# First block: the second half of `down` and the first slot pair after it, run for the context tokens and then for the latent ones

## What is computed

```python
for l in range(2):
    lat = lat + 0.5 * ml[2] * swiglu(modulate(lat, norm_ffn1_g[l], ml[0], ml[1]), *ffn1)
    cx  = cx  + 0.5 * mc[2] * swiglu(modulate(cx,  norm_ffn1_g[l], mc[0], mc[1]), *ffn1)
    # token mixer on modulate(..., norm_mix_g[l], m[3], m[4]): projection w_in (14 slots of
    # 256 columns), gated MLP and bidirectional recurrence, projection w_out, residual
    lat = lat + ml[5] * out_lat        # cx likewise, in layer 0 only
    # second feed-forward like the first; cx in layer 0 only
modulate(x, g, shift, scale) = rmsnorm(x, g) * (1 + scale) + shift
swiglu(h, w1, w3, w2)        = (silu(h @ w1) * (h @ w3)) @ w2
ml[j], mc[j] = the nine parts of silu(cond) @ w_ada[l] + b_ada[l], for latent and context
log_lb, log_rest, kept = logarithms of the recurrence's lower bounds (from two parameter vectors)
```

## Time and profile before

| what | value |
|---|---|
| median of 3 runs | 2869.01 us (2867.65 to 2870.35) |
| profiled execution, its own time | 2868.01 us |
| its span in the trace | 2866.2 us |
| mean granted clock of TensorE | 0.962 of full |
| TensorE busy with matmuls | 2667.0 us (93%), 16745 of them |
| VectorE / ScalarE / POOL busy | 41% / 37% / 24% |
| DMA | 375 MB, mean 131 GB/s |

### The profile page before, as it was taken

One profiled execution on the slowest core, in us unless ns is written; L12 is line 12 of the kernel. 1 busy time (PEld: TensorE's weight loads), 2 busy tenths in 40 slices (PEclk: granted clock), 3 DMA queues, 4 the chain that ended last, 5 costly groups with the idle time before them and its releaser, 6 DMA issues. The chain is left out here.

```text
span 2866.2 us, 42736 instructions
## 1 busy us (share of the span) xinstructions
PE 2667.0 (93%) x16745; PEld 2321.4 (81%) x16745; DVE 1177.1 (41%) x1766; ACT 1068.2 (37%) x1474; POOL 688.5 (24%) x276
## 2 busy tenths in 40 slices
PE   6999898999889999989999989889999589996999
PEld 3888686988868888768888688779989489995999
DVE  3222224237642222242222356743354636634644
ACT  2322233535333222243222346445454344443433
POOL 0222121220012222212222213024434024440343
PEclk8999999999999999989999999999999789997999
DMA  5343353330023333434333424035555025551454
GB/s 228 133 168 138 125 145 114 122 132 1 30 103 139 133 132 132 147 105 145 132 132 132 168 85 162 6 118 176 178 201 190 30 96 180 181 177 44 149 188 148
DMA packets 57279, 375.37 MB, mean 131 GB/s; under 512 B 6159, under 2 KB 10919, under 8 KB 12872
## 3 DMA queue, kind: packets, MB, share of 16 engines
q1 hardware_dynamic: 56092, 371.58, 36.3%
q10 hardware_dynamic: 1068, 2.11, 0.6%
HBM read 370.51 MB, written 3.16 MB: 130 GB/s over the span
## 5 line engine op out<-in xcount | busy, mean ns | idle before, releaser
L1317 POOL TENSOR_TENSOR WL<-RAW,WH 128x1024 fp32r<-128x1024 f32 x272 | 688.3, 2530 | 2164.9 <-ACT WH L972 2164.9
L972 ACT ACTIVATE WH<-RAW 128x1024 fp32r<-128x1024 f32 x544 | 545.6, 1050 | 1075.0 <-PE PSA L512 1067.2
L1340 DVE TENSOR_TENSOR WL<-RAW,WH 128x1024 fp32r<-128x1024 f32 x272 | 346.7, 1275 | 1279.2 <-ACT WH L972 1279.1
L510 PE MATMUL PSA<-HH,WH 128*128 128x256 f32 (+1 forms) x2400 | 817.9, 341 | 25.3 <-DVE HL L1423 23.5
L511 PE MATMUL PSA<-HL,WH 128*128 128x256 f32 (+1 forms) x2400 | 807.9, 337 | 0.0
L512 PE MATMUL PSA<-HH,WL 128*128 128x256 f32 (+1 forms) x2400 | 806.5, 336 | 0.0
L510 PEld LDWEIGHTS PSA<-HH,WH 128*128 128x128 f32 x2400 | 459.8, 192 | 89.9 <-issue 43.2
L510 PE MATMUL PSA<-GH,WH 128*128 128x256 f32 (+1 forms) x1536 | 506.2, 330 | 7.0 <-DVE GL L1358 7.0
L511 PE MATMUL PSA<-GL,WH 128*128 128x256 f32 (+1 forms) x1536 | 498.8, 325 | 0.0
L512 PE MATMUL PSA<-GH,WL 128*128 128x256 f32 (+1 forms) x1536 | 498.5, 325 | 0.0
L512 PEld LDWEIGHTS PSA<-HH,WL 128*128 128x128 f32 x2400 | 459.6, 192 | 46.9
(11 more groups left out here) (254 smaller groups left out, 2207.0 us busy)
## 6 DMA issues: line engine op xcount, KB each, us to landing
RAW<-in_weights SPq DMA_DIRECT2D x272, 1024.0 KB, 4.8
ADA<-in_w_ada SPq DMA_DIRECT2D x65, 1024.0 KB, 4.8
Zada<-in_w_ada SPq DMA_DIRECT2D x7, 1024.0 KB, 13.4
scratch_bias<-BREL ACTq DMA_DIRECT2D x1, 2048.0 KB
SUMS<-in_c_sums SPq DMA_DIRECT2D x1, 1664.0 KB, 8.4
TB<-scratch_bias SPq DMA_DIRECT2D x1, 1536.0 KB, 11.5
X<-in_x SPq DMA_DIRECT2D x1, 1024.0 KB, 8.2
X<-in_ctx SPq DMA_DIRECT2D x1, 1024.0 KB, 12.2
```

The source lines that it names most:

```text
L510: pe.matmul(out, a_hi, b_hi, start=start, stop=False)
L972: act.activation(WH[:, j, 4 * h:4 * h + 4, :], RAW[:, j, 4 * h:4 * h + 4, :], ACT.Copy)\
L1317: pool.tensor_tensor(WL[:, j, 4:8, :], RAW[:, j, 4:8, :], WH[:, j, 4:8, :].bitcast(F32), ALU.subtract)\
L1340: dve.tensor_tensor(WL[:, j, 0:4, :], RAW[:, j, 0:4, :], WH[:, j, 0:4, :].bitcast(F32), ALU.subtract)\
```

## The change

Three parts.

**1.** In a `down` in front of one of the four norms, units 2 and 3 are each run in two halves of 256 tokens: context half of 2, sums of unit 1, context half of 3, context sums of 2, latent half of 2, context sums of 3, latent half of 3, latent sums of 2. The sums go to two banks, one per stream. Each half matmul is 256 tokens wide.

**2.** The norm is made first for the context stream, then for the latent one. On VectorE and ScalarE the evictions of the latent halves, the splits of the next two slots' weights, the squares of the last latent half and the norm's own steps stand in one written order. The first two slots of the next phase run as four halves: context of slot 0, latent sums of unit 3, context of slot 1, latent of slot 0, latent of slot 1.

**3.** The transpose of LBC, its copy and its store become a plan entry `bounds` of their own behind the third `ffn_up`; the bias product stays in `setup`.

The diff, cut to its core:

```diff
@@ plan_slots
+            if l + which == 0 and t == 2:
+                plan.append(dict(kind="bounds"))
...
+    for this in plan:
+        if this["kind"] == "norm":
+            this["by_stream"] = this["tokens"] == 512 and not this["first"]
+    for this, after in zip(plan, plan[1:] + [dict(kind=None)]):
+        this["ends_by_stream"] = after.get("by_stream", False)
+        after["begins_by_stream"] = this.get("by_stream", False)
@@ TensorE
+            def units_by_stream(ph):
...
+                def part(u, s):
+                    j, t = u % 2, streams(512)[s][1]
+                    for m in range(2):
+                        w = slice(P * m, P * m + P)
+                        for kb in range(kin):
+                            if s == 1 and m == 0:
+                                slot_half(ph["slot"] + u, kb)
+                            mm = three(bank(2 * (1 - s) + j)[:, NL * m:NL * m + NL], WH[:, j, kb, w], WL[:, j, kb, w],
+                                       GH[:, kb, t], GL[:, kb, t], kb == 0, kb == kin - 1)
+                    return mm
+                pe.wait_ge(bank_read[0], 2 + ph["unit"] + BANK_CREDIT)
+                part(2, 1).then_inc(part_done, 1)
+                stream_sums(1)
+                if has_ada(ph, 1):
+                    ada_turn(ph, 1)
+                part(3, 1).then_inc(part_done, 1)
+                part_sums(2, 1)
+                if has_ada(ph, 1):
+                    ada_finish(ph, 1)
+                pe.wait_ge(bank_read[1], 2 + ph["unit"] + BANK_CREDIT)
+                part(2, 0).then_inc(mm_done, 1)
+                part_sums(3, 1)
+                part(3, 0).then_inc(mm_done, 1)
+                part_sums(2, 0)
...
+                def pair_by_stream():
...
+                    for j in range(2):
+                        pe.wait_ge(bank_read[j], ph["unit"] + BANK_CREDIT)
+                        half(j, 1)
+                        if j == 0:
+                            part_sums(3, 0)
+                    for j in range(2):
+                        half(j, 0).then_inc(mm_done, 1)
+                        if has_ada(ph, 0):
+                            (ada_finish if j else ada_turn)(ph, 0)
...
                 elif kind == "setup":
 
+                    pe.wait_ge(hot_landed, 32)
+                    pe.matmul(bank(4)[0:8, :], T5[:], HOT[:], start=True, stop=True).then_inc(brel_mm, 1)
+                elif kind == "bounds":
                     pe.wait_ge(lbc_ready, 1)
                     pe.transpose(bank(5)[0:24, 0:P], LBC[:, 0:3, :].rearrange("p q x -> p (q x)"), ident).then_inc(lbr_mm, 1)
-                    pe.wait_ge(hot_landed, 32)
-                    pe.matmul(bank(4)[0:8, :], T5[:], HOT[:], start=True, stop=True).then_inc(brel_mm, 1)
@@ ScalarE
+                squares(2, 1)
+                squares(3, 1)
+                after_slot(down, 1, 0, 2)
+                root(1)
+                squares(2, 0)
+                after_slot(down, 1, 1, 2)
+                high(1, range(0, 4))
+                squares(3, 0)
+                high(1, range(4, KB))
+                root(0)
+                high(0, range(KB))
@@ VectorE
+                dve.wait_ge(part_done, parts + 1)
+                evict(2, 1)
+                rows_copy(down, 1)
+                dve.wait_ge(part_done, parts + 2)
+                evict(3, 1)
+                n.skip(part_done, 2)
+                modulations()
+                dve.wait_ge(mm_done, down["slot"] + 3)
+                evict(2, 0)
+                mean(1, 8)
+                after_slot(down, 1, 0, 2)
...
+                inverse(1)
+                scaled(1, 0)
+                for kb in range(KB):
+                    if kb + 1 < KB:
+                        scaled(1, kb + 1)
+                    if kb == 1:
+                        dve.wait_ge(mm_done, down["slot"] + 4)
+                        evict(3, 0)
+                    lower(1, kb)
+                    if kb == 1:
+                        after_slot(down, 1, 1, 2)
+                mean(0, 4)
+                inverse(0)
```

More of the change, by code:

```diff
@@ L579, in norm @@
                 N = ph["tokens"]
-                early = 0 if ph["first"] else 6
+                early = 0 if ph["first"] else KB if ph["by_stream"] else 6
                 if ph["first"]:
@@ L598, in unit_sums, with stream_sums, part_sums @@
                         column_sums(bank(6)[:, 0:ph["tokens"]], kb == 0, kb == KB - 1, ph["tokens"])
+            def stream_sums(u):
+                for kb in (2 * u, 2 * u + 1):
+                    n.take(sq_ready)
+                    buf = S2[:, n.squares % 2, :]
+                    n.squares += 1
+                    for s, t in streams(512):
+                        mm = pe.matmul(bank(5 - s)[:, 0:NL], ones, buf[:, t], start=(kb == 0), stop=False)
+                    mm.then_inc(sq_used, 1)
+            def part_sums(u, s):
+                for kb in (2 * u, 2 * u + 1):
+                    column_sums(bank(5 - s)[:, 0:NL], False, kb == KB - 1, NL)
+            def units_by_stream(ph):
+                kin = ph["kin"]
+                def part(u, s):
[22 more added lines that the diff above has]
+                part_sums(2, 0)
             def factor_columns():
@@ L669, in weights_phase @@
                     repeat(pe, ph["slots"] // 2, body, loop, first=1)
+                elif ph["begins_by_stream"]:
+                    pair_by_stream()
+                    repeat(pe, ph["slots"] // 2, body, loop, first=1)
+                elif ph["ends_by_stream"]:
+                    body(0)
+                    units_by_stream(ph)
                 else:
@@ L992, in read_out, with norm_by_stream, squares, root @@
                     act.wait_ge(bank_read[p], ph["unit"] + BANK_CREDIT)
+            def norm_by_stream(ph):
+                down = ph["fed_by"]
+                def squares(u, s):
+                    t = streams(512)[s][1]
+                    act.wait_ge(bank_read[1 - s], down["unit"] + BANK_CREDIT + 2 + u - 1)
+                    for m in range(2):
+                        square(NL, X[:, 2 * u + m, t])
+                def root(s):
+                    r = RSTD[:, streams(512)[s][1]]
+                    n.take(var_ready)
+                    act.activation(r, r, ACT.Sqrt).then_inc(std_ready, 1)
+                def high(s, kbs):
+                    t = streams(512)[s][1]
+                    for kb in kbs:
+                        n.take(t_ready)
+                        act.activation(HH[:, kb, t], T2[:, kb % 2, t], ACT.Identity,
+                                       bias=MODS[:, ph["mods"][0], kb, s:s + 1]).then_inc(hh_ready, 1)
+                squares(2, 1)
[9 more added lines that the diff above has]
+                high(0, range(KB))
             def norm(ph):
                 N = ph["tokens"]
+                if ph["by_stream"]:
+                    return norm_by_stream(ph)
                 if ph["first"]:
@@ L1081, in body @@
                                     .then_inc(sq_ready, 1)
+                if ph["ends_by_stream"]:
+                    body(0)
+                    n.squares += KB // 2
+                    return
                 repeat(act, 2, body, ph is not PLAN[-1])
@@ L1300, in _ @@
             handlers = {"norm": norm, "ffn_up": ffn_up, "mlp_up": mlp_up, "down": down, "w_in": w_in, "in_even": in_proj,
-                        "in_odd": in_proj, "mixer": mixer, "setup": setup}
+                        "in_odd": in_proj, "mixer": mixer, "setup": setup, "bounds": bounds}
             for ph in PLAN:
```

81 lines of the change are left out of this document (75 added, 6 removed).

## The result

| | before | after |
|---|---|---|
| median | 2869.68 us (4 runs, 2867.65 to 2872.99) | 2838.58 us (4 runs, 2837.60 to 2839.06) |
| profiled execution, its own time | 2868.01 us | 2839.06 us |
| four windows at the norms, together | 258.2 us | 239.8 us |
| set-up: from the start of the last `ada_finish` before it to the end of slot 0 | 23.26 us | 12.50 us |
| all the rest of the profiled execution | 2586.6 us | 2586.8 us |

The ratio is 0.9888, 95% interval [0.9875, 0.9900]: 1.1% faster, 31 us by the medians and 29.0 us by the two profiled executions. The forecast was 2844 us with a range of 2831 to 2856. The last line of the table makes these two profiles easy to read against each other: outside the places that the change touches they agree to 0.2 us.

A forecast was written before the change was run, and what follows sets the result against it. TensorE, busy 93% of the span, was taken as the bound, with time won only where it waits or runs at half clock. 2868.0 - 14.6 (norms) - 10.4 (set-up) = 2843.0, median 1.0 above: 2844 us, range 2831 to 2856.

The forecast's parts named there:

- The norm by stream without the clock: At the four norms, counted from unit 2's first matmul: windows of 61.0, 60.6, 56.2 and 61.0, together 238.8 us.
- the held HL 0: First context block of a norm: POOL's weight split delays VectorE's HL, which ends at 27.3 instead of 25.5 us.
- The clock: In the four norm windows: the fall to 1.2 GHz comes back and costs 1.2 us a norm, 4.8 in all.
- The bounds of 0 to 3.4 us a norm: In the norm windows: the least and most that the half clock could cost each norm.
- The set-up: From the last `down` before it to slot 0's end: no LBC wait, full clock, transpose moved; gain 10.4 us.
- The cost of halving: In the units and `ffn_up` pairs: 0.013 us per former 512-wide matmul, 6.6 us for 504 more matmuls.
- the Trainium skill's figure, 2839 us: For the 504 more matmuls: about 2.5 ns fixed cost each, 1.3 us instead of 6.6, so about 2839 us.
- POOL does hold HL 0: Rival at the norms claimed POOL does not hold HL up: each norm ends 1.8 us earlier, 2837 us; chance 0.12.
- The norms did give back: Rival claimed the norms give nothing back and only the set-up counts: 2858.6 us; chance 0.13.
- slot 2 of the next phase never waited for its weights: After the pair of slots: slot 2's weight split just fits into 7.3 us; waiting there would show the forecast wrong.
- TensorE did not stay at half clock: Rival at the norms claimed sparse groups keep TensorE at 1.2 GHz through all four halves: 2907 us; chance 0.04.
- The bias product had no wait of its own: Rival at the set-up claimed the bias matmul has a wait that the LBC wait hid: 2852 us; chance 0.05.

The follow-up runs named there:

- keep-warm run: The changed kernel plus matmuls nobody reads, 8 before the context half of slot 0 and 2 each before its blocks 1 and 2: 2839.56 us, ratio 0.9885.
- second trace: The changed kernel measured again, with no edit, beside later runs: 2839.14 us, ratio 0.9887, four windows 239.3 us.

## Why the prediction was right

- **The norm by stream without the clock.** Worked out: 61.0, 60.6, 56.2 and 61.0, 238.8 us. Measured: 61.08, 60.22, 55.92 and 62.56, 239.8, with a clock that was not full; at full clock 237.8 by the keep-warm run. The worked sum was 1 us too long (60.6 and 56.2 for windows of 60.16 and 55.94, most of it). The start of the context half (27.3 against 27.5), the held HL 0 (forecast about 2.5 us, 2.27), the end of the context half of slot 0 (39.0 against 38.9), the last latent block (50.4 against 50.5) and the end of slot 1 (61.0 against 61.1) came where the sum put them. This rests on the one norm of 256 tokens in the trace of before, whose pace of 0.92 us a block returned unchanged.
- **The clock** was the term of the wrong size: 4.8 us were put down for the four norms, and it took 1.9 us (1.4 in the second trace). With the 1 us above, the norms gave 18.4 us instead of 14.6. The fall itself came (mean clock 0.89 to 0.97). What failed is the 1.2 us a norm: at half clock the paced blocks before `w_in` still fit into their pace, and only the fourth norm, where the low stretch reached dense work, paid 1.6 us. Before `ffn_up` it was only 6.8 and 3.4 us long, and the context half of the second window ended 0.1 us later than at full clock. The bounds of 0 to 3.4 us a norm hold it.
- **The set-up.** 10.4 us forecast, 10.8 measured (22.90 to 12.14): wait, clock and bias product as worked out; the transpose costs 0.03 us on the path and not 0.39, since the next matmul starts in its pipeline.
- **The cost of halving** by the rows was right: in the trace after, matmuls at full clock start 0.120 us apart at 256 tokens and 0.227 at 512, as before, which is 0.013 us for each one halved. The third window, nearest to full clock, was put at 56.2 us and took 55.92. The 2.5 ns of the Trainium skill ("TensorE: Matmul & The Clock Gate", in "Wait — 56ns, not 53.3ns?") would make the steps 0.109 and 0.216 us, an estimate from its figure. The measurement decides against it here, where a weight load stands beside every matmul (402 of each in the first window). "The weights change with every matmul" is not quite right: the first two matmuls of `three` have the same stationary operand, which is loaded again. That the sum with the Trainium skill's figure, 2839 us, is the time that came (2838.58) is coincidence: the 5.3 us between it and the forecast are about what the clock term, the worked sum, the set-up and the spread of the kernel before make up.
- **The rivals.** POOL does hold HL 0, and with HH first it held T of block 3 instead. The norms did give back; slot 2 of the next phase never waited for its weights. TensorE did not stay at half clock (3.4 to 13.7 us a window). The bias product had no wait of its own.
- **The sum.** Forecast 25.0 us from the two terms; 29.2 us as measured, 29.0 between the profiled executions. The remaining 2 us between the medians' 31.1 and that lie within the spread of the kernel before, whose runs reach from 2867.65 to 2872.99. The measured time is 5 us under the forecast, inside its range.

Not tried: taking POOL out of the two splits at a norm, which would show what the hold costs in full; by HL 0's 2.27 us for 0.48 it is 1.8 us a norm at most, an estimate. Open is what sets the length of a low stretch of the clock: the same kernel had 13.7 us in one trace and 6.8 in another in its fourth window.

## What to carry to other kernels

Where a reduction over all features stands between two products, halving the tokens lets one half's norm run beside the other half's product; sum it up from a norm of that size in the same trace, chain by chain, and include what the other engines do in the meantime. After such a change the next gains lie in the written order: look for the operation that is much longer than its equals and see which engine it overlaps, and put the sums that a chain waits for ahead of work that nobody waits for. A wait in a set-up can be worth more than its length, since the work behind it may run at half clock: here 7.57 us of wait gave 10.8 us. Before filling idle time to keep the clock up, look whether the work behind it is dense; work paced by another engine hides the half clock.

## What the runs showed of the hardware

- The hold between VectorE and POOL acts on single operations in both directions: HL 0.48 to 2.27 us, T 0.48 to 2.56 us, POOL's subtraction 2.34 to 3.18 us. Evictions with one PSUM input (0.88 us for two) and the reciprocal (1.75 us) ran beside POOL at their usual length.
- Twelve products that nobody reads kept the granted clock at 1.00 through three norms of four. The mean clock of a window does not tell its cost: 0.94 cost 0.1 us where the low stretch met paced blocks, and 0.97 cost 1.3 us where it met matmuls back to back.
- The issue of a small store right behind another store on ScalarE's queue took 14.61 us, and 0.38 us when it stood 68 us later. No run shows what in the first store caused it.
- A small transpose between matmuls of other shapes delays the next one by 0.03 us although its own row says 0.27.
